# Down products of the loop's expert and of the first expert behind it in the split form

## The reference, cut to what matters

```python
def hier_moe(h, ...):                    # 768 tokens of 1024
    ...                                  # group, then the top two of its four experts, gates
    for e in range(N_EXPERTS):           # 16
        gu = t @ w_gate_up[e]            # 1024 x 512
        y = (jax.nn.silu(gu[:, :256]) * gu[:, 256:]) @ w_down[e]     # 256 x 1024
        out = out + combine[:, e:e + 1] * y
```

## Time and profile before

| | us |
|---|---|
| median of three runs (603.07 to 603.18) | 603.16 |
| the profiled execution | 603.42 |
| its span on the core | 601.6 |
| TensorE busy | 593.8 |
| VectorE busy | 417.6 |
| ScalarE busy | 330.3 |

### The profile page before, as it was taken

One profiled execution on the slowest core, in us unless ns is written; L12 is line 12 of the kernel. 1 busy time (PEld: TensorE's weight loads), 2 busy tenths in 40 slices (PEclk: granted clock), 3 DMA queues, 4 the chain that ended last, 5 costly groups with the idle time before them and its releaser, 6 DMA issues.

```text
span 601.6 us, 8723 instructions
## 1 busy us (share of the span) xinstructions
PE 593.8 (99%) x3160; PEld 490.6 (82%) x3160; DVE 417.6 (69%) x773; ACT 330.3 (55%) x595; POOL 68.1 (11%) x109
## 2 busy tenths in 40 slices
PE   8999999999999999999999999999999999999997
PEld 6888989888887777888887887778888888878886
DVE  5426962344542666746877789899999999788863
ACT  7752200322232675656555566799999998961211
POOL 0060000000000000100100114142121220210000
PEclk9999999999999999999999999999999999999999
DMA  8916655120312412212314778989999999785611
GB/s 333 404 34 229 236 220 205 36 95 10 102 38 71 183 36 106 87 54 106 106 72 154 248 246 296 405 316 414 411 410 411 412 412 376 290 314 198 227 42 64
DMA packets 39042, 126.52 MB, mean 210 GB/s; under 512 B 6448, under 2 KB 7472, under 8 KB 38968
## 3 DMA queue, kind: packets, MB, share of 16 engines
q1 hardware_dynamic: 33224, 112.97, 50.4%
q0 software_dynamic: 4896, 12.59, 5.4%
q10 hardware_dynamic: 880, 0.41, 0.2%
HBM read 113.33 MB, written 23.10 MB: 227 GB/s over the span
## 4 chain that ended last, share of the span: by engine, by line
PE 93%; DMA 2%; DVE 2%; ACT 1%; issue 1%; SPq 0%; DVEq 0%; POOLq 0%; POOL 0%; ACTq 0%
PE bank L509 21%; PE bank L511 20%; PE bank L510 20%; PE bank L1958 7%; PE bank L540 6%; PE bank L541 6%; PE bank L539 5%; PE bank L1975 3%; PE bank L1994 3%; PE bank L2109 2%; PE bank L2268 1%; DMA moe_rows<-moe_y,slot_row 1%; DMA pick<-moe_rows 1%; DMA colv<-in_cols 1%; DVE w_split L1733 0%
## 5 line engine op out<-in xcount | busy, mean ns | idle before, releaser
L504 DVE TENSOR_TENSOR w_split<-w_raw,w_split 128x1024 fp32r<-128x1024 f32 x33 | 40.5, 1228 | 22.5 <-ACT w_split L499 22.3
L509 PE MATMUL bank<-w_split,moe_xT 128*128 128x512 f32 x120 | 48.4, 404 | 0.8 <-DVE w_split L1733 0.8
L1023 ACT ACTIVATE sq_tmp<-bank 128x512 f32<-128x512 f32 x12 | 7.2, 599 | 75.5 <-PE bank L511 75.5
L511 PE MATMUL bank<-w_split,moe_xT 128*128 128x512 f32 x120 | 47.0, 391 | 0.0
L510 PE MATMUL bank<-w_split,moe_xT 128*128 128x512 f32 x120 | 46.8, 390 | 0.0
L499 ACT ACTIVATE w_split<-w_raw 128x1024 fp32r<-128x1024 f32 x33 | 34.7, 1054 | 18.9 <-PE bank L541 16.6
L988 ACT ACTIVATE s<-s,mn 128x512 f32<-128x512 f32 (+1 forms) x48 | 30.9, 645 | 18.7 <-DVE mn L1441 18.7
L488 DVE TENSOR_TENSOR w_split<-w_raw_more,w_split 128x1024 fp32r<-128x1024 f32 x32 | 37.9, 1216 | 2.7 <-ACT w_split L482 2.2
L509 PE MATMUL bank<-w_split,x3T 128*128 128x512 f32 (+1 forms) x104 | 39.5, 379 | 0.2 <-DVE x3T L1907 0.2
L511 PE MATMUL bank<-w_split,x3T 128*128 128x512 f32 (+1 forms) x104 | 38.8, 373 | 0.0
L510 PE MATMUL bank<-w_split,x3T 128*128 128x512 f32 (+1 forms) x104 | 38.8, 373 | 0.0
(11 more groups left out here) (329 smaller groups left out, 1592.1 us busy)
## 6 DMA issues: line engine op xcount, KB each, us to landing
w_raw<-in_w_moe SPq DMA_DIRECT2D x32, 512.0 KB, 5.5
w_raw_room<-in_w_moe SPq DMA_DIRECT2D x30, 512.0 KB
w_raw_more<-in_w_moe SPq DMA_DIRECT2D x30, 512.0 KB
w_raw<-in_w_in SPq DMA_DIRECT2D x23, 512.0 KB
pick<-moe_rows SPq DMA_DIRECT2D x12, 512.0 KB, 4.8
bias_rows<-bias_table SPq DMA_DIRECT2D x1, 4096.0 KB
w_raw<-in_w_out SPq DMA_DIRECT2D x8, 512.0 KB
toep<-bias_rows SPq DMA_DIRECT2D x4, 896.0 KB, 7.1
```

Source lines behind the costliest of these rows:

```text
L504: nc.vector.tensor_tensor(W[:, u % WS, 1], raw(u)[0], f(W[:, u % WS, 0]), ALU.subtract).then_inc(lo_done, 1)
L509: nc.tensor.matmul(out, hi, whi, start=first, stop=False)
L511: return nc.tensor.matmul(out, hi, wlo, start=False, stop=last)
```

## The change

The down product of the loop's tile and that of block 1 take the split form.
- ScalarE makes the high parts of units 4 and 5: in the loop ahead of those of units 0 to 2, in block 1 unit 4 behind (2, 3) and ahead of the activation, unit 5 behind the activations' high part. The plain copies of the activations become their high part.
- VectorE makes the low parts of units 4 and 5 and of the activations.
- TensorE has `down_hi` (four matmuls, the activations' high part with both parts of the weights) and `down_lo` (two matmuls with the activations' low part), per half.
- The loop's count of low parts goes from four to six a pass. SyncE requests units 4 and 5 when their low parts are made and no longer when TensorE has used them; the same for (4, 4) and (4, 5).

The diff, cut to its core:

```diff
@@ SyncE
             with sp.Fori(0, n) as i:
                 src = expert(i + 1)
                 for j in range(4):
-                    sp.wait_ge(lp_lo, i * 4 + (j + 5))
+                    sp.wait_ge(lp_lo, i * 6 + (j + 7))
                     set_unit(src, j)
                 src = expert(i)
                 for j in range(4, 6):
-                    sp.wait_ge(lp_y, i * 2 + (j - 3))
+                    sp.wait_ge(lp_lo, i * 6 + (j + 1))
                     set_unit(src, j)
...
             for j in range(4, 6):
-                sp.wait_ge(pe_y, j - 3)
+                sp.wait_ge(lp_lo, n * 6 + (j + 1))
                 moe_unit((4, j))
@@ ScalarE
             with act.Fori(0, n) as i:
+                for j in range(4, 6):
+                    loop_hi(i, j)
                 for j in range(3):
                     act.wait_ge(lp_used, i * 3 + (j + 1))
                     loop_hi(i, j)
                 act.wait_ge(lp_gu, i + 1)
                 out_silu(0).then_inc(lp_si, 1)
                 act.wait_ge(lp_at, i + 1)
-                act.activation(act32[:], bank[3][:, 0:DE].rearrange("p (k t) -> p k t", k=2),
-                               ACT.Copy).then_inc(lp_aat, 1)
+                out_actT_hi(actT).then_inc(lp_aat, 1)
...
             moe_hi((2, 3))
+            loop_hi(n, 4)
             silu(1)
             moe_hi((3, 0))
             moe_hi((3, 1))
-            act.wait_ge(pe_aT2, 1)
-            act.activation(act_first[:], bank[3][:, 0:DE].rearrange("p (k t) -> p k t", k=2),
-                           ACT.Copy).then_inc(a_aT2, 1)
+            actT_hi(1)
+            loop_hi(n, 5)
             moe_hi((3, 2))
@@ VectorE: the rows stand below
@@ TensorE
-            def raw_down(half, a, done):
-                w = RAW[:, (MOE0 + 4 + half) % RS]
+            def down_hi(half):
+                w = W[:, WSLOT[1, 4 + half]]
+                for part in range(2):
+                    for k in range(2):
+                        pe.matmul(bank[4 + half][:], actT[0][:, k], w[:, part, k],
+                                  start=(part == k == 0), stop=False)
+
+            def down_lo(half, done):
+                w = W[:, WSLOT[1, 4 + half]]
                 for k in range(2):
-                    ins = pe.matmul(bank[4 + half][:], a[:, k], w[:, k], start=(k == 0), stop=(k == 1))
+                    ins = pe.matmul(bank[4 + half][:], actT[1][:, k], w[:, 0, k], start=False, stop=(k == 1))
                 ins.then_inc(done, 1)
...
                 for half in range(2):
                     pe.wait_ge(lp_aat, i * 2 + (half + 1))
-                    pe.wait_ge(lp_ld[4 + half], i * 16 + 16)
-                    raw_down(half, act32, lp_y)
+                    pe.wait_ge(lp_lo, i * 6 + (half + 5))
+                    down_hi(half)
+                    pe.wait_ge(lp_act, i * 2 + 2)
+                    down_lo(half, lp_y)
```

More of the change, by code:

```diff
@@ L225, in build @@
                      for j, o_ in enumerate((0, 4096, 40960, 8192))]
-        act32 = sb("loop_actT", [P, 2, P], F32, "X")
         x_first = sb("moe_x_first", [P, D], F32, "R1", 4096)
@@ L233, in build @@
         actT_last = [sb(f"moe_last_actT{i}", [P, 2, P], F32R, "R2", 1024 * i) for i in range(2)]
-        act_first = sb("moe_first_actT", [P, 2, P], F32, "R1", 1024)
         sg = sb("moe_silu", [P, DE], F32, "R1", 2048)
@@ L1818, in _ @@
             with dve.Fori(0, n) as i:
-                loop_lo(i * 4 + 5, 0)
+                loop_lo(i * 6 + 5, 4)
                 dve.wait_ge(lp_si, i + 1)
                 out_act(0).then_inc(lp_act, 1)
-                for j in range(1, 4):
-                    loop_lo(i * 4 + (j + 5), j)
+                loop_lo(i * 6 + 6, 5)
+                dve.wait_ge(lp_aat, i * 2 + 1)
+                out_actT_lo(actT).then_inc(lp_act, 1)
+                for j in range(4):
+                    loop_lo(i * 6 + (j + 7), j)
                 for half in range(2):
@@ L1833, in _ @@
             act_mul(1)
-            for j in range(3):
+            loop_lo(n * 6 + 5, 4)
+            for j in range(2):
                 moe_lo((3, j))
+            actT_lo(1)
+            loop_lo(n * 6 + 6, 5)
+            moe_lo((3, 2))
             def late_hots():
@@ L2273, in unit_split @@
                 if t == 1:
-                    pe.wait_ge(lp_lo, n * 4 + (j + 1))
+                    pe.wait_ge(lp_lo, n * 6 + (j + 1))
                 else:
@@ L2289, in down @@
                 if t == 1:
-                    pe.wait_ge(a_aT2, 1)
+                    pe.wait_ge(d_aT2, 1)
                     pe.wait_ge(lp_ay, n * 2)
                     for half in range(2):
-                        pe.wait_ge(lp_ld[4 + half], n * 16 + 16)
-                        raw_down(half, act_first, pe_y)
+                        unit_split(1, 4 + half)
+                        down_hi(half)
+                        down_lo(half, pe_y)
                     return
-                pe.wait_ge(d_aT2, t - 1)
+                pe.wait_ge(d_aT2, t)
                 for half in range(2):
@@ L2307, in _ @@
                 for j in range(4):
-                    pe.wait_ge(lp_lo, i * 4 + (j + 1))
+                    pe.wait_ge(lp_lo, i * 6 + (j + 1))
                     up_unit(0, j, WSLOT[1, j]).then_inc(lp_used if j < 3 else lp_gu, 1)
@@ L2311, in _ @@
                 ple_proj(5, (1,), (0,))
-                pe.wait_ge(lp_act, i + 1)
+                pe.wait_ge(lp_act, i * 2 + 1)
                 turn(bank[3], act_t, 2, lp_at)
```

## The result

| | median, us | lowest to highest | runs |
|---|---|---|---|
| before | 603.06 | 602.38 to 603.18 | 6 |
| changed | 608.51 | 606.74 to 609.37 | 6 |

The account below looks back on a forecast made before the run. It took TensorE's own work to bound the kernel, with VectorE having 0.47 us of slack. TensorE's 1.58 us saving vanishes behind VectorE's chain, +2.6 us in all, giving 605.8 us against the 603.16 median; range 604.4 to 607.0.

Parts of the forecast that it names:

- The down passes: TensorE, loop and first block: twelve split matmuls, 2.74 us, replace 3.53 us of float32; saves 0.79 us each, 1.58 in all.
- The loop: VectorE's 2.6 us of extra work fits 3.4 us of idle time; tokens' low part still starts at 381.65.
- SyncE's request: Loop's later low parts delay SyncE's queue by 2.0 us; unit 4 requested at 383.2 instead of 381.2.
- The landing of unit 4: First block's weights land at 388.3, between 387.3 and 388.7, with queued units at 410 GB/s, 1.28 us each.
- rival 4: Unit 4 lands later still, at 390.1, with the 6.9 us of today's unit 5: 4.4 us lost, 607.5; chance 0.07.
- From landing to tokens: First block: VectorE takes 10.31 us without idle time from product (389.75) to third block's tokens (400.06), against 8.18 before.
- second pause: TensorE waits about 3.1 us for the third block's tokens; its stream starts 2.6 us later than 397.55.
- VectorE's chain: First block: VectorE's added work, started late by unit 4's weights, sets the end: 605.8 us; chance 0.60.
- The first pause: First block: TensorE wants the product's result at 389.5 and gets it at 390.2, a pause of 0.7 us.
- No second loss: Behind the third block's start at 400.2, everything runs as today, only 2.6 us later.
- Rival 5: TensorE's 3.1 us pause drops its clock to 1.2 GHz, costing 2.0 us more: 607.8; chance 0.03.

Follow-up runs that it names:

- run 3: Changed kernel with the split form in the loop alone, first block's down pass in plain float32 as before: 602.74 us, ratio 0.9995.
- run 2: Changed kernel with SyncE requesting the loop's units 4 and 5 ahead of the next set's units 0 to 3: 605.94 us, ratio 1.0058.
- 6: Changed kernel with 20 constant matmuls filling TensorE's second pause, ahead of the third block: 607.82 us, ratio 1.0088.
- 7: Changed kernel with constant matmuls in both TensorE pauses (14 and 20) and gathers from block 5's on one block earlier: 607.35 us, ratio 1.0067.
- run 5: Kernel before, with VectorE computing the low parts of (3,0) and (3,1) twice: 604.65 us, ratio 1.0028.
- version 4: Split form in the first block alone, the loop as in the kernel before: 606.33 us, ratio 1.0050.
- run 8: On top of run 2, GpSimd's gathers from block 5's on issued one block earlier: 605.98 us, ratio 1.0045.
- run 9: On top of run 2, the second block's activation on VectorE moved ahead of two low parts: 606.22 us, ratio 1.0045.

## Why the prediction was too small

- *The down passes.* Forecast -0.79 us each; 2.85 instead of 3.53 in the loop, -0.68. I had taken the start-up behind the transposes (0.09) off the new form only, and it is there in both. Right in kind, and of no consequence, since it vanished into a pause as forecast.
- *The loop.* VectorE's tokens start at 381.65 as worked out, TensorE waits for nothing in it, and the loop's split alone costs nothing (run 3). Right.
- *SyncE's request.* Worked out: 383.2; it was issued at 383.2. That a large part of the price lies in the order of SyncE's queue was right: run 2 got back 2.6 us by that order alone.
- *The landing of unit 4.* **This term failed.** Forecast 388.3, bounds 387.3 to 388.7; it came at 389.7 to 390.8. The first unit behind the dry queue took 4.5 us instead of 4.1, and the four that follow with the stored rows 6.7 us (383.0 to 389.7) instead of 5.8 (by its own terms the forecast adds up to 388.4). Units 0 to 2 land 1.25 us apart, at the forecast pace; unit 3 comes 2.7 us behind unit 2 in this profile, where 1.28 and the 0.7 of the stored rows were reckoned. I had taken 410 GB/s from slices in which the queue was long full. The windows of the changed kernel:

```profile
378.00:380.00 2.00, 2.00 (x12) 1.64 (x11) 2.00 (x3) 1.24 (x3) 0.00 (x0) 1.00 0.96 287
380.00:382.00 2.00, 2.00 (x14) 1.74 (x12) 2.00 (x3) 2.00 (x4) 0.69 (x1) 1.00 0.93 311
382.00:384.00 2.00, 2.00 (x14) 1.71 (x13) 2.00 (x4) 2.00 (x3) 0.62 (x1) 1.00 1.03 369
384.00:386.00 2.00, 2.00 (x12) 1.67 (x11) 2.00 (x4) 2.00 (x4) 0.00 (x0) 1.00 0.79 250
```

  The last number is GB/s: 304 on average, so 1.72 us for a unit of 0.524 MB, not 1.28. In the kernel before the same four stretches show 395 to 422. All profiles agree: from 378 to 386 us the five in which SyncE asks for nothing between 372 and 378 us (both of the changed kernel, 3, 6 and 7) average 257 to 331 GB/s, and the nine others 384 to 407. Why the low rate lasts so long behind the first new request no run here shows. The prediction's own rows had the 6.9 us of today's unit 5, and I gave rival 4, which used it, 0.07. It was nearer than my 388.3.
- *From landing to tokens.* Forecast 10.31 us from product to tokens and 3.1 us of second pause; 10.22 and 2.98. The mechanism, VectorE's chain, was right, and run 5 shows it by itself: 604.65 against 604.5. The first pause was 1.8 instead of 0.7, from the late landing (1.4) less the 0.2 by which TensorE itself came later than worked out.
- *No second loss.* Right for what I had looked at: from the stream's start to the transposes of block 4's tokens 5.88 us at full clock, 5.73 before, and the blocks behind it keep their 9.3 us. I had not asked what a later and denser VectorE does to GpSimd's transfers; in version 2 that gave a wait of 1.1 us.
- *The clock.* **Wrongly weighed.** Rival 5 was worked out in the prediction (2.0 us) and given 0.03, for want of a row with a pause of this length. The clock fell in 8 of 11 runs, at 1.3 us by the two profiles of the changed kernel, 1.6 by those of 4, 8 and 9, and 2.0 by the runs of version 4, of which one alone was at full clock. A pause of 3 us behind a kernel that never paused for more than 0.8 deserved half the chance, and it adds to each of the other cases and is no alternative to them.

Put together: the transposes of block 4's tokens are 4.0 us later (407.24 against 403.28), which on the median of before gives 607.0 at full clock for the earliest of the landings seen. Up to 1.1 us more come from a later one, and 1.3 or more from the clock in most runs: the median of 608.5 lies inside. By the runs, the three of the changed kernel at full clock lie at 606.7 to 608.2 us, the eight at the lower one at 607.5 to 609.4, with medians of 607.7 and 608.5. The late landing alone takes the full-clock time to the top of the stated range and over it, and the clock adds the rest.

One difference is not the change's: the 4.0 us still stand at the transposes of block 14's tokens (500.44 against 496.48), but the spans differ by 3.3. From there to the end it takes 105.1 us in the profile before and 104.5 here. In all fourteen profiles it lies between 104.3 and 105.5 us, without order by kernel, so this is no sign that the late waits of the earlier trace rows gave anything back. What I can't settle is the share of each term in a single run that has no profile, and why the landings spread over 1.1 us.

## What to carry to other kernels

When a change moves work from the engine that bounds to one with little slack, look for the next hand-over between them and add up the second engine's row there: 0.47 us of slack was the whole answer to a saving of 1.58. Trace each wait that a queue of requests takes on, with all that is queued behind it, and do not price a transfer that starts in an emptied queue by the rate of a full one. Before crediting an edit with a wait that went away, check that the awaited thing came earlier and not the waiting engine later (run 8). And a forecast pause of TensorE longer than any in the profile is a cost of its own on top of its length: here one of 1.4 us kept the clock, and those of 2.2 to 3.0 us lost it in most runs.

## What the runs showed of the hardware

- *Pauses and the clock:* the table above, from 0 of 8 runs at 1.4 us to 12 of 15 at 2.5 us, with matmuls at 0.43 us instead of 0.23 behind the pause, and a loss of 1.3 to 1.6 us in four profiles (2.0 by the runs of version 4). Filling the pauses with 34 small matmuls on constants (4.1 us of work) kept the clock in all 5 runs.
- *A queue that starts anew:* 257 to 331 GB/s on average over the 8 us from 378 us on in the five profiles with a pause of SyncE's requests before them, against 384 to 407 in the nine without. That the two go together is shown; the mechanism is not.
- *GpSimd's indirect transfers under VectorE:* 1.0 us each beside an idle VectorE or at its instructions on a bank, and up to 4.67 us beside its chain of low parts, whose operands both lie in SBUF. The long ones end 0.9 to 1.0 us behind a start or an end of a VectorE instruction, all but one of 3.26 us in 8. The Trainium skill (SBUF — State Buffer, SBUF: two separate sides) has VectorE with two SBUF inputs and a GpSimd operation that reads SBUF exclude each other over a shared port pair. These transfers take their row numbers from SBUF, the traces agree with the page as far as the delay goes (1.0 against 4.67 us), and run 9 moved the end of such a transfer by moving one VectorE instruction; that the port is the cause is not shown.
